# Moving a first context product, a split step and four weight loads in a two-layer trunk kernel

## What is computed

```
def ec_moe(h, p):                       # once for the context rows, once for the latent rows
    cap = EC_FACTOR * n // N_EXPERTS    # 128 latent rows, 16 context rows per expert
    aff = softmax(xt @ router)
    gate, idx = top_k(aff.T, cap)
    xe = take(xt, idx)
    hid = silu(xe @ w_gate) * (xe @ w_up)
    ye = (hid @ w_down) * gate
    out = zeros.at[idx].add(ye)

x = x + g1 * mixer(modulate(rms_norm(x, norm1), sh1, sc1))
x = x + g2 * ec_moe(modulate(rms_norm(x, norm2), sh2, sc2))
# sh1, sc1, g1, sh2, sc2, g2 = split(silu(cond) @ ada_w + ada_b): the conditioning
```

## Time and profile before

| | us |
|---|---|
| median of 3 runs | 3453.77 (3443.75 to 3455.03) |
| profiled execution | 3448.96 |
| its span | 3446.9 |
| TensorE busy | 3191.7 (93%) |
| VectorE busy | 2244.0 (65%) |
| ScalarE busy | 1871.6 (54%) |
| GpSimd busy | 587.3 (17%) |

### The profile page before, as it was taken

How to read it: one execution, slowest core, us unless ns; L and a number is a source line. 1 busy time by engine, 2 the same in 40 slices (tenths; PEclk the granted TensorE clock), 3 DMA queues, 4 the chain that set the end, 5 groups by cost and what they waited for, 6 DMA issues and landing times. The chain is left out here.

```text
span 3446.9 us, 55218 instructions
## 1 busy us (share of the span) xinstructions
PE 3191.7 (93%) x19994; PEld 2426.5 (70%) x19994; DVE 2244.0 (65%) x2850; ACT 1871.6 (54%) x2649; POOL 587.3 (17%) x455
## 2 busy tenths in 40 slices
PE   6988989997999999998898999999897899999999
PEld 3547777784676767675787888888885567676766
DVE  3557676545666666665677676867756666666666
ACT  3454646522565666563457383754733456566654
POOL 1001010000223332221211112011100133222231
PEclk9989999997999999999999999999997999999999
DMA  7230000146888888887110100100045688888885
GB/s 244 82 107 20 1 22 1 57 153 255 313 296 291 298 289 294 283 303 222 50 41 8 41 1 8 41 7 22 24 162 201 220 294 294 290 291 287 300 288 160
DMA packets 214169, 565.35 MB, mean 164 GB/s; under 512 B 33699, under 2 KB 71272, under 8 KB 213736
## 3 DMA queue, kind: packets, MB, share of 16 engines
q1 hardware_dynamic: 203614, 529.21, 43.0%
q0 software_dynamic: 9472, 33.57, 4.1%
q10 hardware_dynamic: 906, 0.23, 0.0%
HBM read 524.00 MB, written 38.94 MB: 163 GB/s over the span
## 5 line engine op out<-in xcount | busy, mean ns | idle before, releaser
L1880 DVE TENSOR_TENSOR moe_lo<-moe_raw,moeg_hi 128x2048 fp32r<-128x2048 f32 x384 | 880.4, 2327 | 314.4 <-PE psum L2228 154.9
L1877 ACT CAST moeg_hi<-moe_raw 128x2048 fp32r<-128x2048 f32 x384 | 728.9, 1910 | 417.0 <-PE psum L2246 293.8
L949 PE MATMUL psum<-attn_w_hi,attn_hs 128*128 128x256 f32 (+2 forms) x1440 | 377.1, 346 | 25.4 <-DVE attn_hs L1304 11.3
L1428 DVE TENSOR_REDUCE attn_neg_max<-psum 128x1 f32<-128x1280 f32 (+1 forms) x216 | 292.5, 1356 | 88.2 <-PE psum L1054 87.9
L1214 ACT ACTIVATE attn_e<-psum,attn_neg_max 128x1280 f32<-128x1280 f32 (+1 forms) x216 | 265.4, 1229 | 78.4 <-DVE attn_neg_max L1428 59.9
L1054 PE MATMUL psum<-attn_ks,attn_qst 128*128 128x512 f32 (+2 forms) x1200 | 285.1, 371 | 17.2 <-ACT attn_qst L1151 6.5
L949 PEld LDWEIGHTS psum<-attn_w_hi,attn_hs 128*128 128x128 f32 x1440 | 256.7, 192 | 56.8 <-DVE attn_hs L1304 18.3
L2246 PE MATMUL psum<-moeg_hi,moeh_x_hi 128*128 128x512 f32 x960 | 265.7, 399 | 4.8 <-issue 4.8
L2246 PE MATMUL psum<-moe_lo,moeh_x_hi 128*128 128x512 f32 x960 | 262.8, 395 | 0.0
L2246 PE MATMUL psum<-moeg_hi,moeh_x_lo 128*128 128x512 f32 x960 | 260.4, 393 | 0.0
L1054 PEld LDWEIGHTS psum<-attn_ks,attn_qst 128*128 128x128 f32 x1200 | 212.2, 191 | 63.9 <-issue 12.3
(11 more groups left out here) (312 smaller groups left out, 5329.3 us busy)
## 6 DMA issues: line engine op xcount, KB each, us to landing
moe_raw<-in_l_w_gate SPq DMA_DIRECT2D x256, 512.0 KB, 4.0
moe_raw<-in_l_w_up SPq DMA_DIRECT2D x256, 512.0 KB, 5.1
moe_raw<-in_l_w_down SPq DMA_DIRECT2D x128, 1024.0 KB, 6.2
ada_w<-in_l_ada_w SPq DMA_DIRECT2D x23, 1024.0 KB, 13.6
lru_ada<-in_l_ada_w SPq DMA_DIRECT2D x16, 1024.0 KB, 7.4
ada1h_w<-in_l_ada_w SPq DMA_DIRECT2D x9, 1024.0 KB, 11.4
out_w<-in_l_w_out SPq DMA_DIRECT2D x16, 512.0 KB, 5.5
h_rows<-mix_xs SPq DMA_DIRECT2D x16, 512.0 KB, 2.7
```

Source lines behind the costliest of these rows:

```text
L949: last = pe.matmul(out, hs[t % 2][:, part, k, :], right, start=(i == 0 and n == 0), stop=(i == KB - 1 and n == 2))
L1428: dve.tensor_reduce(neg_max[:, n:n + 1], m.psum[:, score_at(n):score_at(n) + hi - lo], AX.X, ALU.max, negate=True).then_inc(s["maxed"], 1)
L1877: act.copy(mm.hi[slot % 4][:, :, :], mm.raw[slot][:, :, :]).then_inc(mm.s["hi_ready"], 1)
L1880: dve.tensor_tensor(mm.lo[slot][:, :, :], mm.raw[slot][:, :, :], mm.hi[slot % 4][:, :, :].bitcast(F32), ALU.subtract).then_inc(mm.s["lo_re ...
```

## The change

Three things are moved. First, in layer 1's routing, half 0 of the first context product goes ahead of the turning of the lists, half 1 stays behind it. In layer 0, half 0 moves from the experts into routing, behind the turned lists, and the high part of slot 0 moves with it to the end of ScalarE's routing program. Second, in layer 1 VectorE's low part of slot 0 waits for a new semaphore, which a one-element memset on Pool raises behind the gather's issue. Third, at the tail of layer 0's experts, tables and the first conditioning load go out together with the attention weights, and the other three each when `lat_done` is 186, 187 and 188, all ahead of the last `store_yc`. The slots are put in another order, so that the load that needs no freed slot comes first. `mm.n_high` is set and read nowhere.

```
@@ routing, gpsimd
             mm.gather(pool, dram)
+            pool.memset(pair[0:1, 0, 0:1], 0.0).then_inc(s["gather_issued"], 1)
@@ routing, tensor
+            def first_ctx_gu():
+                pe.wait_ge(mm.s["padded"], 1)
+                pe.wait_ge(mm.s["xc_ready"], 1)
+                mm.ctx_gu(pe, 0, 0)
...
                 last.then_inc(s["g2_spread"], 1)
+            if l == 1:
+                first_ctx_gu()
             pe.wait_ge(s["topped"], 2)
             pe.transpose(m.psum[:, 4 * BANK:4 * BANK + EXP], topf[0:EXP, 0:CAP_L], m.ident[0:EXP, 0:EXP])
...
                         ).then_inc(s["top_turned"], 1)
-            if l == 1:
-                pe.wait_ge(mm.s["padded"], 1)
-                pe.wait_ge(mm.s["xc_ready"], 1)
-                for half in range(2):
-                    mm.ctx_gu(pe, 0, half)
+            mm.ctx_gu(pe, 0, 1) if l == 1 else first_ctx_gu()
@@ routing, scalar
             if l == 1:
                 act.wait_ge(mm.s["ctx_done"], 2)
                 mm.copy_gu_c(act)
+            else:
+                act.wait_ge(mm.loaded[0], 32)
+                mm.copy_high(act, 0)
@@ routing, vector
+            if l == 1:
+                dve.wait_ge(s["gather_issued"], 1)
             for k in range(mm.n_low):
@@ experts, sync
-            tail_loads[0](sp)
+            tail_loads(sp, 0)
...
             sp.dma_start(mm.y_all[0:filled, :, :], y_rows[0:filled, :, :]).then_inc(s["y_all_loaded"], 16)
+            for n in range(1, 4):
+                sp.wait_ge(s["lat_done"], UNITS * EXP - 7 + n)
+                tail_loads(sp, n)
             store_yc(LAST)
             sp.wait_ge(s["yc_stored"], 64 * EXP)
             sp.dma_start(mm.y_all[filled:P, :, :], y_rows[filled:P, :, :]).then_inc(s["y_all_loaded"], 16)
-            tail_loads[1](sp)
-            sp.wait_ge(s["lat_done"], UNITS * EXP - 4)
-            tail_loads[2](sp)
             sp.wait_ge(s["ctx_added"], 2)
@@ experts, tensor
             turn_x(0)
-            if l == 0:
-                ctx_gu(0, 0)
@@ experts, scalar
-            if l == 0:
-                high(0, 32, None)
@@ build
-                         for i, at in enumerate((9 * 8192, 10 * 8192, 11 * 8192, 124576))]
+                         for i, at in enumerate((124576, 9 * 8192, 10 * 8192, 11 * 8192))]
...
+            def tail_loads(sp, n):
+                if n == 0:
+                    attn_pre[1].load(sp, 0)
+                    attn_pre[1].load_tables(sp)
+                norm_ada.ahead(sp, n, n + 1)
```

## The result

The changed kernel is slower by a small amount: 3460.11 us median over 20 runs (3456.15 to 3465.81), beside 3453.53 us for the kernel before over 20 runs of the same session (3443.75 to 3457.79). The ratio is 1.0021, with a 95% interval of 1.0014 to 1.0028, so 4.8 to 9.7 us more. The difference is inside the 0.3% band that the prediction called "within". The time itself is just outside the range (3459). The forecast was a net gain of 1 us from two parts of opposite sign; the part that costs was about twice as large as it was taken.

The account below looks back on a forecast made before the run. It took TensorE to bound the kernel through the layer-1 experts. Terms -4.5 + 0 + 3.5 = -1.0 us gave 3448.0 from the profiled execution, 3452.8 from the median; forecast 3450 us, range 3440 to 3459.

Parts of the forecast that it names:

- Part 3: Tail of layer 0's experts: the last context rows land late behind moved loads; 3.5 us lost, bounds 0.7 and 6.6.
- The sum: First, the tail's landing estimate, 1625.0; in bold, the whole forecast: -4.5 + 0 + 3.5 = -1.0 us, so 3448.0 us.
- the 20.5 us of busy engines: Layer-0 experts' tail, 1612.0 to 1632.5: DMA engines busy with tables, four loads, two scatters and the context store.
- Rival B: Layer-0 tail: slower by the last rows' landing, deciding from 1626.0 us; at 1628.5 it costs +2.5 net; chance 0.17.
- Part 1: Layer-1 routing: first context half runs ahead of the list turns, under VectorE's list making; gain 4.5 us, at most 4.9.
- The bound by which the memset retires only with Pool's drain: Layer-1 routing: memset retires at 2680.4, low part ends at 2682.7, stage starts at 2683.5; gain 2.5 us.
- rival C: Layer-1 routing: the memset holds VectorE; -2.5 + 3.5 = +1, 3451 us; chance 0.08.
- Part 2: Layer-0 experts' head: first latent product 2.9 us earlier, cold, then eaten by loads; 0, bounds 1.4 gain, 2.5 loss.
- A: Layer-0 tail: the small store isn't held up, stage ends 4.7 us earlier; -9.2 in all, or 3441 us; chance 0.13.
- D: Layer-1 routing: half 1 can't start earlier, Pool sets the stage start, clock stays cold; 2.6 us left, 3451; chance 0.05.

Follow-up runs that it names:

- experiment 2: The kernel before with only the new tail order of layer 0's experts: 3461.48 us, ratio 1.0023.
- experiment 3: The changed kernel with the last store of context rows, its reload and the context store issued from ScalarE's queue: 3452.53 us, ratio 1.0001.
- experiment 9: The changed kernel with the old tail order and one low part instead of two in layer 1's routing: 3451.63 us, ratio 0.9994.
- experiment 10: The kernel before with only layer 0's first context half and slot 0's high part moved into routing, run twice: 3456.56 and 3455.57 us.
- experiment 1: The changed kernel with the old tail order, tables and all four loads behind the last store and reload: 3450.80 us, ratio 0.9989.
- experiment 5: The changed kernel with the old tail order, but the four conditioning loads behind the context store: 3451.44 us, ratio 0.9997.
- experiment 4: The changed kernel with the last store and its reload ahead of conditioning loads 1 to 3: 3450.13 us, ratio 0.9986.
- 11: The kernel before with the layer-1 routing changes and the last store and reload ahead of loads 1 to 3, layer-0 head unchanged: 3449.03 us, ratio 0.9984.

## Why the prediction was wrong

**Part 3 is the step that failed, by its size.** The mechanism was the one forecast: the last stores wait behind 4 MB, TensorE idles, placing runs cold, the context store then lands quickly. I took 3.5 us with bounds of 0.7 and 6.6; it was 7.8 (after), and 7.9 by the ratio of experiment 2. Term by term, put on the time axis of before (3.7 us ahead of after's: 1617.28 against 1620.95):

| | taken | measured |
|---|---|---|
| landing of the last context rows | 1625.0 (at most 1626.5) | 1627.8 |
| reload to placing | 2.0 | 2.5 |
| placing, cold | 5.6 | 6.33 |
| end of placing to the issue of the context store | 1.5 | 1.5 |
| context store | 2.6 | 2.6 |

The largest miss, 2.8 us, is the landing. The sum took the 20.5 us of busy engines, subtracted 5.2 for two scatters and added one back: 14.0 us for tables and loads, 2.6 for a scatter. In the new order both scatters went out while the stores were on their way, at 1613.43 and at 1626.98, ahead of the landing at 1631.42. The shares of the DMA engines from the first store's issue to the reload (after, 1612.53 to 1631.42, 18.89 us: packets, MB, share; q1 is SP's queue, q0 the scatters) put a size to it:

```profile
q1 hardware_dynamic: 2162, 4.81, 80.9%
q0 software_dynamic: 222, 0.84, 23.8%
```

That is 4.5 us of the engines' time for scatters instead of 2.6, and 15.3 for SP's queue instead of 14.0: the second scatter counts, but not whole, since it was still moving when the stores landed (from 1630.5 to 1631.4 only q0 moved bytes, 0.18 MB). No run took a scatter away. The sum also treated the stores as transfers only, and missed that SP itself is held while it issues them (11.13 us for four). In experiment 3, with the same loads under way, the four on another queue were issued in 1.88 us, and the reload followed 8.8 us behind the first of them instead of 18.9. How much of these 10 us is the held issue and how much the place behind the loads, no run tells. The cold placing was put between 3.60 and 7.2; behind 13 us of idle time it ran at the low clock (0.50 in 1634 to 1636) for most of its length, so the upper end was the nearer one. Rival B had this mechanism with the right sign ("by the last rows' landing", deciding from 1626.0). It was given 0.17 and a price of +2.5 net. Its objection, that the 20.5 us already held both scatters, was the wrong one.

**Part 1**: forecast a gain of 4.5 us, bounds 2.5 and 4.9; measured 3.2. One half was taken off the path as said, and the half behind the turned lists was cold. Only its duration was off: 6.36 us, not 5.1. I worked with 5.1 to 6.4 and took the early end, although the slices had the clock rise between 2680 and 2681, 5.1 to 6.1 us behind the product's start (for the 3 us of my early end no row stands), and the trace of before had the duration itself: both halves behind the same gap took 9.66 us, a warm one takes 3.64, so the cold one took 9.66 - 3.64 = 6.02. Before, too, it was the half right behind the gap that ran cold. The change takes away the warm one, worth at most 3.64, and the cold one grew by 0.34: 3.3, and 3.2 was measured. The clock stood at 0.50 from 2692 to 2694, 3.5 to 5.5 us into the half. The idle time ahead of it, 3.18 us, was as forecast (3.3). Pool's drain took 4.76 us (forecast 4.85), the memset 0.09 (estimated 0.3). The order of who ends the stage was right: TensorE with ScalarE's copy, then VectorE and Pool. The bound by which the memset retires only with Pool's drain, and rival C with it, are wrong here: the low parts start at 2690.18, 3.4 us ahead of that drain's end. The Trainium skill's caution on Pool's spans ("Perfetto Trace Analysis", "GPSIMD Engine Instruction") says that they are unreliable, not that a memset waits for a drain; that step was mine, and the trace does not bear it out. I missed that a second low part was added; it cost nothing (experiment 9).

**Part 2**: forecast 0, with the first latent product 2.9 us earlier, cold, and the rest eaten by the loads. It came 2.2 us earlier, cold (2.04 us instead of 1.16), and 3.0 us earlier in the executions whose routing was as short as in the trace of before (experiment 10). After's wait for the load became shorter (0.56 instead of 1.87 us), not longer, but the length of the routing goes with that: with a long routing the wait was 0.61 us without part 2 as well (experiment 2). With a short one it was 1.5 to 2.8 us with part 2 (six executions) and 0.6 and 1.9 without. The total agrees with 0.

**Rivals.** A (the small store isn't held up) is refuted by the 8.2 us and 11.13 us. D (part 1 without effect, 2.6 us at the least) came nearer than I gave it credit for: a half that stayed cold almost throughout left 3.2.

**The sum** with the measured terms is 7.8 - 3.2 + 0 = +4.6 us, 3458.1 from the median of 3453.5. The remaining 2.0 us to 3460.11 stay open. Two things bear on them. Stages that the change doesn't touch were longer in after's profile, and stage lengths come in two groups from kernel to kernel, whatever their code: the layer-0 routing was at 51.4 to 51.7 us or at 54.5 to 56.4, with the new code and with the old, the layer-1 attention at 828.7 to 830.5 or 831.7 to 832.4. And part 1, worth 3.2 us in its stage, shows about 1.4 in the totals. Neither was settled. The intervals would allow for the 2.0 us: experiment 1 differs from after by the tail alone, and the ratios are 0.0032 apart, 11 us, with 0.0007 and 0.0009 on either side, or about 4 us for the difference, which takes in the 7.8 that the tail costs.

## What to carry to other kernels

A small store on which a reload and then a product depend must not stand behind bulk loads on the same queue; price it by the bytes ahead of it (here 3.5 us per MB), add the cold clock of the engine that waits, and count the loads' cost at each dependent step and not only at the first. Loads that the next stage needs at once are paid for on one side of the boundary or the other (experiment 5); the orders with the lowest ratios among those tried with all of them on one queue had the short dependent transfers first and the loads right behind them (4 and 11, though from the old order with the other parts, experiment 1, they can't be told). When work behind an idle gap is split and one half moved ahead of the gap, what is won is the warm price of that half, since the other half is the cold one, and was so before. And a gain or loss at the head of a stage is put down to the change only between executions whose preceding stage was equally long.

## What the runs showed of the hardware

- SP's issue can be held. Four 16 KB stores took 11.13 and 11.04 us to issue behind all 4.5 MB that were moved, and 1.73 both with none of it and with 1.5 MB ahead; on ScalarE's queue, beside the same loads, 1.88. A trace shows this as a long DMA row on the queue, not as a wait.
- A queue of its own doesn't escape the traffic: 16 KB landed in 7.3 us (1.8 on quiet engines), 512 KB in 8.7 us (2.6 on quiet engines, 11.2 behind the loads on SP's queue, 6.2 with the loads issued right behind it on that queue).
- The gather's issue took 1.05 us alone and 3.00 us beside two low parts on VectorE (inputs and output in SBUF), and Pool's drain behind it 4.76 and 6.65 us.
- TensorE's clock at one place differs between executions of one and the same code: the gate spread in 3.82 or 6.13 us. Behind the gap of 3.2 to 3.5 us in layer 1 the second half began cold in all ten kernels that had it (6.15 to 6.37 us instead of 3.64); placing behind a gap of 2.52 us (experiment 4) wasn't cold (3.70).
